# The gates of the experts: scaled one-hot rows made by GpSimd in one step, and the row of numbers read from PSUM by VectorE

## The chip, the cores and the metric

One Trainium2 chip, one core of it. The metric is the device time of one execution in microseconds. The times given are of whole executions; the trace is of one execution more, with its own time beside it.

## What is computed

The program is two blocks of a transformer one after the other, all in float32, for 256 tokens of width 1024. The change lies in the second block, which has two layers. Each ends with a layer of experts: 128 x 128 keys give 16384 experts, and every token picks, for each of 8 heads, 16 of them. From the picks a gate for each token and expert follows.

```python
def peer_ffn(xn, wq, subkeys, u_tab, v_tab):
    ...
    i1 = jnp.take_along_axis(top_i[..., 0, :], ci // PEER_TOPK, axis=-1)
    i2 = jnp.take_along_axis(top_i[..., 1, :], ci % PEER_TOPK, axis=-1)
    idx = i1 * PEER_N_KEYS + i2
    g = jax.nn.softmax(best, axis=-1)
    ...
        act = jax.nn.gelu(jnp.einsum('ckd,cd->ck', u_tab[ic], xc), approximate=False)
        return jnp.einsum('ck,ckd->cd', (gc * act).astype(v_tab.dtype), v_tab[ic])
```

So a token has 8 x 16 = 128 picks, each with a first key, a second key and a weight. The kernel computes every expert's activation and multiplies it by a gate that is the weight where the expert was picked and zero elsewhere.

## The kernel before

Every engine runs its own fixed list of instructions in the order written; semaphores order the engines against each other. A layer of the second block is a `Mixer` and a `Peer`. In `Peer`, these steps follow one another: the norm and the projections of the queries; the scores against the 128 keys of each half; `EarlyScores`, in which TensorE computes the activations of the first 33 of 128 tiles of experts while VectorE runs `Route` (the sixteen best, and the picks); `Gates`; and `Experts`, the long loop over 128 tiles of 128 experts.

`Route` leaves in the tile `slots` three numbers of each pick: with the 128 picks on the partitions and the 256 tokens along a row, `slots[:, 0, n]` is the weight, `slots[:, 1, n]` the first key and `slots[:, 2, n]` the second key of token n.

`Gates` turns them into a matrix of 128 x 128 gates for each token, one matmul per token. For token n it needs two tiles of 128 picks by 128 numbers: `first`, which has a one where the number is the pick's first key, and `second`, which has the weight where the number is the pick's second key. Their product over the picks is the token's gates. Four tokens make a group, whose four products fill one bank of PSUM (banks 0 to 3 in turn); there are 64 groups in a layer, 128 in all. `second` lies in a part of `hT` that is not otherwise in use (the context's half), so that its rows are named hT in the profile. For each group g:

- VectorE, in `make`, compares the row of numbers `iota` (0 to 127, in SBUF) with the second keys of the four tokens (L2441, 128x512) and with the first keys (L2443, 128x512), two instructions.
- ScalarE, in `scale`, multiplies each of the four tokens' rows of `second` by the weight, in place (L2463, four instructions of 128x128).
- TensorE multiplies (L2422; each of the four matmuls in float32 stands as two rows in the trace).
- ScalarE, in `move_late`, moves the gates of 95 of the 128 tiles of experts to `gates` (L2470, 128x380, from PSUM).
- VectorE, in `weigh_early`, multiplies the activations of the first 33 tiles with their gates, read from PSUM (L2449, 128x132).

VectorE's list is make(g), weigh_early(g - 2), and ScalarE's is move_late(g - 2), scale(g). make(g) waits for the products of group g - 4, which used the same one of four buffers; weigh_early(g) waits for move_late(g). GpSimd does nothing in `Peer`; its work is in the attention of the first block (L1239) and in the mixers (L1511, L1602 and others), and its lines for a mixer come before and after it. `Experts` begins on VectorE and ScalarE when the last gates are moved and weighed. Bank 4 was last used for the scores against the keys, and is used next for the sums of `Experts`.

Of the kernel before, what the change touches and what calls it, by code (L numbers as in the profile page):

```python
# [10 lines left out]
ACT = mybir.ActivationFunctionType  # L11
ALU = mybir.AluOpType
AX = mybir.AxisListType

P = 128
# [33 lines left out]
class Span:  # L49


    def __init__(self, sem, first):
        self.sem, self.first = sem, first
# [17 lines left out]
class Use:  # L71
# [3 lines left out]
    def __init__(self, tensor, written, read):  # L75
        self.tensor, self.written, self.read = tensor, written, read
# [11 lines left out]
class Bank:  # L88
    def __init__(self, tensor, written, read):
        self.tensor, self.written, self.read = tensor, written, read  # L90
# [75 lines left out]
def hold(engine, marks):  # L166

    for sem, count in marks:
        engine.wait_ge(sem, count)
# [107 lines left out]
class Fetch:  # L277
# [7 lines left out]
    def scalar(self, after=()):  # L285
        hold(self.nc.scalar, after)
        for dst, src in self.pairs:
            self.nc.scalar.dma_start(dst, src).then_inc(self.landed.sem, 16)
# [7 lines left out]
class Setup:  # L296
# [5 lines left out]
    def vector(self):  # L302
        nc, k = self.k.nc, self.k
        nc.vector.memset(k.ones[:], 1.0).then_inc(self.made.sem, 1)
        nc.vector.memset(k.eps, EPS).then_inc(self.made.sem, 1)
        nc.vector.memset(self.silu[:], 0.0).then_inc(self.made.sem, 1)


class Modulation:
# [35 lines left out]
    def tensor(self, step):  # L345
        k, pe, (g, c) = self.k, self.k.nc.tensor, divmod(step, DC)
        use = self.rows[g]
        if step == 0:
            pe.wait_ge(*self.silu_made.after(1))
        if c == 0:  # L350
            pe.wait_ge(*use.free())
        units = [k.ring.take_whole() for _ in range(2)]
        for b in range(4):
            m = pe.matmul(use.tensor[32 * b:32 * b + 32, :], self.silu[:, c, :],  # L354
                          units[b // 2][:, (b % 2) * 512:(b % 2 + 1) * 512], start=(c == 0), stop=(c == DC - 1))
            if b % 2:
                m.then_inc(k.ring.used, 1)
# [412 lines left out]
class Projection:  # L770


    def __init__(self, k, w, tiles, cuts, x, width, place, arrive=None, b0=0, scale=lambda t: 1.0, between=None):
        self.scale, self.between = scale, between
        self.k, self.w, self.tiles, self.cuts, self.x, self.width = k, w, list(tiles), cuts, x, width
        self.place, self.arrive = place, arrive
        self.first_half = 0
        self.uses = [k.bank[b0 + n % 4].use(written=0) for n in range(len(self.tiles))]
        self.done = [u.emptied() for u in self.uses[-2:]]
# [276 lines left out]
class PairAttention:  # L1056
# [175 lines left out]
    def gpsimd(self):  # L1232
        pool = self.k.nc.gpsimd
        for s in range(len(self.steps)):
            n = self.keys(s)
            pool.wait_ge(*self.den.after(s + 1))
            for u in range(2):
                p = self.prob[:, s % 3, u, 0:n]
                pool.tensor_scalar(p, p, self.rec[:, s % 4, u:u + 1], 1.0, ALU.mult,  # L1239
                                   ALU.mult).then_inc(self.weighed.sem, 1)  # L1240
# [1154 lines left out]
class Gates:  # L2395
# [5 lines left out]
    def __init__(self, k, slots, iota, early, gates, first, second, routed):  # L2401
        self.routed = routed
        self.k, self.slots, self.iota, self.early, self.gates = k, slots, iota, early, gates
        self.first, self.second = first, second
        self.uses = [k.bank[g % 4].use() for g in range(self.GROUPS)]
        self.second_made = k.named("second_key_rows").take(self.GROUPS)
        self.first_made = k.named("first_key_rows").take(self.GROUPS)
        self.scaled = k.named("rows_scaled").take(self.GROUPS)
        self.moved = k.named("gates_moved").take(self.GROUPS)
        self.done = [u.emptied() for u in self.uses[-4:]] + [self.moved.after(self.GROUPS)]  # L2410

# [3 lines left out]
    def tensor(self):  # L2415
        pe = self.k.nc.tensor
        for g, use in enumerate(self.uses):
            pe.wait_ge(*self.first_made.after(g + 1))
            pe.wait_ge(*self.scaled.after(g + 1))
            pe.wait_ge(*use.free())  # L2420
            for t in range(4):
                m = pe.matmul(use.tensor[:, t * P:(t + 1) * P], self.first[:, g % 4, t, :], self.rows(g, t),  # L2422
                              start=True, stop=True)
            m.then_inc(use.written.sem, 1)

    def vector(self):
        hold(self.k.nc.vector, self.routed)
        for g in range(self.GROUPS + 2):
            if g < self.GROUPS:
                self.make(g)  # L2430
            if g >= 2:
                self.weigh_early(g - 2)

    def make(self, g):
        dve = self.k.nc.vector
        row_no = self.iota[:].unsqueeze(1).to_broadcast([P, 4, P])
        tokens = slice(4 * g, 4 * g + 4)
        keys = [self.slots[:, j, tokens].unsqueeze(2).to_broadcast([P, 4, P]) for j in (1, 2)]
        if g >= 4:
            dve.wait_ge(*self.uses[g - 4].full())  # L2440
        dve.tensor_tensor(self.second[g % 4], row_no.rearrange("p (c k) n -> p c k n", c=2),  # L2441
                          keys[1].rearrange("p (c k) n -> p c k n", c=2), ALU.is_equal).then_inc(self.second_made.sem, 1)
        dve.tensor_tensor(self.first[:, g % 4], row_no, keys[0], ALU.is_equal).then_inc(self.first_made.sem, 1)  # L2443

    def weigh_early(self, g):
        dve, use = self.k.nc.vector, self.uses[g]
# [3 lines left out]
                          ALU.mult).then_inc(use.read.sem, 1)  # L2450

    def scalar(self):
        for g in range(self.GROUPS + 2):
            if g >= 2:
                self.move_late(g - 2)
            if g < self.GROUPS:
                self.scale(g)

    def scale(self, g):
        act = self.k.nc.scalar  # L2460
        act.wait_ge(*self.second_made.after(g + 1))
        for t in range(4):
            m = act.activation(self.rows(g, t), self.rows(g, t), ACT.Copy,  # L2463
                               scale=self.slots[:, 0, 4 * g + t:4 * g + t + 1])
        m.then_inc(self.scaled.sem, 1)

    def move_late(self, g):
        act, use = self.k.nc.scalar, self.uses[g]
# [169 lines left out]
class Peer:  # L2638
# [38 lines left out]
    def tensor(self):  # L2677
        pe = self.k.nc.tensor
        self.normed.tensor()
        self.q1.tensor()  # L2680
        self.q2.tensor()
        hold(pe, self.fetch.done + self.q1.done + self.q2.done)
        for tt in range(2):
            for g, use in enumerate(self.key_uses[tt]):
                pe.wait_ge(*use.free())
                for j in range(4):
                    n = 4 * g + j
                    m = pe.matmul(use.tensor[:, j * P:(j + 1) * P], self.qT[:, n, tt * P:(tt + 1) * P],
                                  self.subkeys[:, n, :], start=True, stop=True)
                m.then_inc(use.written.sem, 1)  # L2690
        self.scored.tensor()
        self.route.tensor()
        self.gate.tensor()
        self.experts.tensor()

    def scalar(self):
        act = self.k.nc.scalar
# [23 lines left out]
class Program:  # L2721
# [56 lines left out]
    def gpsimd_program(self):  # L2778
        self.even.gpsimd()
        self.odd.gpsimd()  # L2780
        for layer in self.layers[0::2]:
            layer.gpsimd()


# [153 lines left out]
```

## Time and profile before

| | |
|---|---|
| time, median of 3 executions | 3473.45 us (3460.08 to 3475.53) |
| time of the execution that was profiled | 3467.66 us |
| its span, first to last instruction | 3466.1 us |
| TensorE busy | 3180.4 us, 92% of the span |
| VectorE busy | 2029.0 us, 59% |
| ScalarE busy | 1648.6 us, 48% |
| GpSimd busy | 111.2 us, 3% |
| chain of work that ended last | TensorE 87%, VectorE 6%, issue 4%, ScalarE 3% |

In the rows further on PE is TensorE (PEld its weight loads), DVE is VectorE, ACT is ScalarE and POOL is GpSimd. A row of a group of instructions gives its line in the kernel, the engine, the operation, the names of output and inputs, the shapes, the count, the total busy time in us and the mean duration of one in ns; behind the last bar stands the engine's idle time before them and what ended it. In a timeline the first number is the start from the span's beginning and the second how long the row lasted, both in us.

### The profile page before, as it was taken

What the parts mean: (1) busy time and instruction counts of PE and PEld (TensorE: products, weight loads), DVE (VectorE), ACT (ScalarE), POOL (GpSimd) and SP (SyncE); (2) the same over time, 40 slices, a digit from 0 to 9 for tenths busy, and PEclk for the clock granted to TensorE, in tenths of its full rate; (3) what the DMA queues carried; (4) which work ended last, traced back from release to release, by engine and by line L of the source; (5) the groups of instructions that cost most, each with busy time, mean ns of one, the idle gap of its engine ahead of it and who ended that gap; (6) DMA issues with size and microseconds to landing.
All of it is one profiled execution on the core that took longest, in us unless ns stands there. A gap on an engine that the chain in (4) does not pass through costs nothing.

```text
span 3466.1 us, 50181 instructions
## 1 busy us (share of the span) xinstructions
PE 3180.4 (92%) x18944; PEld 2700.9 (78%) x18944; DVE 2029.0 (59%) x4174; ACT 1648.6 (48%) x3566; POOL 111.2 (3%) x176
## 2 busy tenths in 40 slices
PE   7998999997899878996899999988799679999999
PEld 4745677776799767985789999978698568999998
DVE  2233433335665665689666666657569876666665
ACT  2244322223655335319655555543441875555554
POOL 0022000000200020000000000001100000000000
PEclk9989999998999878999999999989699999999999
DMA  5501444432155313440355655543144025555654
GB/s 212 182 1 68 158 170 169 157 106 80 50 185 178 136 62 95 155 135 1 128 186 187 187 185 188 187 158 111 36 166 152 31 72 185 187 184 188 188 183 152
DMA packets 135055, 479.85 MB, mean 138 GB/s; under 512 B 15520, under 2 KB 17440, under 8 KB 134048
## 3 DMA queue, kind: packets, MB, share of 16 engines
q1 hardware_dynamic: 132944, 471.26, 41.6%
q10 hardware_dynamic: 1872, 5.38, 0.4%
q8 instruction: 153, 2.51, 0.3%
q14 instruction: 86, 0.70, 0.1%
HBM read 475.53 MB, written 1.05 MB: 137 GB/s over the span
## 4 chain that ended last, share of the span: by engine, by line
PE 87%; DVE 6%; issue 4%; ACT 3%; DMA 1%; ACTq 0%; DVEq 0%; SPq 0%
PE psum L763 15%; PE psum L765 14%; PE psum L764 14%; PE psum L2577 7%; PE psum L2579 7%; PE psum L2578 7%; PE psum L2498 7%; PE psum L2422 4%; PE psum L853 2%; PE psum L1112 2%; PE psum L354 1%; PE psum L613 1%; PE psum L1122 1%; PE psum L627 1%; DVE a_scaled L728 1%
## 5 line engine op out<-in xcount | busy, mean ns | idle before, releaser
L248 DVE TENSOR_TENSOR w_lo<-raw,w_hi 128x512 fp32r<-128x512 f32 x1440 | 971.3, 691 | 788.2 <-ACT w_hi L239 760.0
L239 ACT ACTIVATE w_hi<-raw 128x512 fp32r<-128x512 f32 x1440 | 875.1, 625 | 823.2 <-PE psum L765 450.1
L763 PE MATMUL psum<-x_hi,w_hi 128*128 128x256 f32 x2032 | 581.6, 286 | 3.6 <-DVE x_lo L679 3.6
L765 PE MATMUL psum<-x_hi,w_lo 128*128 128x256 f32 x2032 | 580.1, 285 | 0.0
L764 PE MATMUL psum<-x_lo,w_hi 128*128 128x256 f32 x2032 | 576.9, 284 | 0.0
L2577 PE MATMUL psum<-w_hi,wt_hi 128*128 128x512 f32 x1024 | 407.5, 398 | 6.5 <-DVE wt_lo L2635 6.5
L2579 PE MATMUL psum<-w_hi,wt_lo 128*128 128x512 f32 x1024 | 406.0, 396 | 0.0
L2578 PE MATMUL psum<-w_lo,wt_hi 128*128 128x512 f32 x1024 | 405.2, 396 | 0.0
L763 PEld LDWEIGHTS psum<-x_hi,w_hi 128*128 128x128 f32 x2032 | 389.1, 191 | 12.1 <-issue 4.0
L764 PEld LDWEIGHTS psum<-x_lo,w_hi 128*128 128x128 f32 x2032 | 391.9, 193 | 8.0
L765 PEld LDWEIGHTS psum<-x_hi,w_lo 128*128 128x128 f32 x2032 | 387.5, 191 | 0.0
L763 PE MATMUL psum<-a_hi,w_hi 128*128 128x512 f32 (+1 forms) x880 | 310.4, 353 | 17.7 <-DVE a_lo L735 16.3
L765 PE MATMUL psum<-a_hi,w_lo 128*128 128x512 f32 (+1 forms) x880 | 305.5, 347 | 0.0
L764 PE MATMUL psum<-a_lo,w_hi 128*128 128x512 f32 (+1 forms) x880 | 304.2, 346 | 0.0
L2579 PEld LDWEIGHTS psum<-w_hi,wt_lo 128*128 128x128 f32 x1024 | 193.9, 189 | 46.7
L2498 PE MATMUL psum<-xn,u_raw 128*128 128x256 f32 x1056 | 228.2, 379 | 0.0
L2577 PEld LDWEIGHTS psum<-w_hi,wt_hi 128*128 128x128 f32 x1024 | 193.4, 189 | 44.7 <-DVE wt_lo L2635 6.9
L2578 PEld LDWEIGHTS psum<-w_lo,wt_hi 128*128 128x128 f32 x1024 | 194.3, 190 | 38.3
L2422 PE MATMUL psum<-hT,first 128*128 128x128 f32 x1024 | 147.9, 289 | 82.4 <-issue 76.7
L763 PEld LDWEIGHTS psum<-a_hi,w_hi 128*128 128x128 f32 x880 | 168.5, 192 | 70.0 <-issue 37.8
L2498 PEld LDWEIGHTS psum<-xn,u_raw 128*128 128x128 f32 x1056 | 200.5, 190 | 27.2
L2422 PEld LDWEIGHTS psum<-hT,first 128*128 128x128 f32 x1024 | 127.4, 196 | 103.2 <-issue 96.9
(312 smaller groups left out, 4432.3 us busy)
## 6 DMA issues: line engine op xcount, KB each, us to landing
raw<-in_v SPq DMA_DIRECT2D x256, 512.0 KB, 4.4
raw<-in_u SPq DMA_DIRECT2D x190, 512.0 KB, 3.4
raw<-in_mod_w SPq DMA_DIRECT2D x96, 512.0 KB, 4.4
raw<-in_w_gate_up SPq DMA_DIRECT2D x88, 512.0 KB, 4.9
u_raw<-in_u SPq DMA_DIRECT2D x66, 512.0 KB, 3.4
raw<-in_w_in SPq DMA_DIRECT2D x40, 512.0 KB, 3.5
raw<-in_w_down SPq DMA_DIRECT2D x32, 512.0 KB, 3.5
raw<-in_w_peer SPq DMA_DIRECT2D x32, 512.0 KB, 4.2
```

What stands on the lines that cost most here:

```text
L239: self.nc.scalar.activation(self.hi[:, m % 4, :], self.half(m), ACT.Copy).then_inc(self.rounded[m % 4], 1)
L248: self.nc.vector.tensor_tensor(self.lo[:, m % 4, :], self.half(m), self.hi[:, m % 4, :], ALU.subtract).then_inc(self.ready[m % 4], 1)
L763: pe.matmul(out[:, 0:width], hi[:, w], x_hi, start=(c == 0), stop=False)
L764: pe.matmul(out[:, 0:width], hi[:, w], x_lo, start=False, stop=False)
L765: mm = pe.matmul(out[:, 0:width], lo[:, w], x_hi, start=False, stop=(c == total - 1))
L853: m = pe.matmul(use.tensor[:, 0:self.width], w[:, c * P:(c + 1) * P], self.x(c), start=(c == 0), stop=(c == DC - 1))
L1112: m = pe.matmul(use.tensor[:, 0:n], both[u][j][0], both[u][j][1], start=(j == 0), stop=(j == last))
L2422: m = pe.matmul(use.tensor[:, t * P:(t + 1) * P], self.first[:, g % 4, t, :], self.rows(g, t), start=True, stop=True)
L2498: m = pe.matmul(use.tensor[:, 0:LAT], self.raw[:, t % 3, c * P:(c + 1) * P], self.xn[:, c, :], start=(c == 0), stop=(c == DC - 1))
L2577: pe.matmul(out, self.wt_hi[:, s, rows], hi, start=(t == 0), stop=False, skip_group_check=True)
L2578: pe.matmul(out, self.wt_hi[:, s, rows], lo, start=False, stop=False, skip_group_check=True)
L2579: m = pe.matmul(out, self.wt_lo[:, s, rows], hi, start=False, stop=(t == NKEY - 1), skip_group_check=True)
```

## The change

The kernel's three uses of the row of numbers are made in other places. `second` is made and scaled by GpSimd: one `tensor_scalar` for each token, which compares `iota` with the token's second key and multiplies by its weight, both taken as one number per partition. VectorE keeps the comparison for `first`, and reads the row of numbers from bank 4 of PSUM, where TensorE puts it once in a layer, by a matmul with the identity, ahead of the transposes of `Route`. ScalarE's `scale` is gone, so its list in `Gates` is move_late alone. GpSimd's waits are those of `make`: for `slots` at the start, and for the products of group g - 4.

```diff
@@ class Gates
         self.uses = [k.bank[g % 4].use() for g in range(self.GROUPS)]
+
+        self.numbers = k.bank[4].use(read=self.GROUPS)
         self.second_made = k.named("second_key_rows").take(self.GROUPS)
-        self.first_made = k.named("first_key_rows").take(self.GROUPS)
-        self.scaled = k.named("rows_scaled").take(self.GROUPS)
...
         for g, use in enumerate(self.uses):
-            pe.wait_ge(*self.first_made.after(g + 1))
-            pe.wait_ge(*self.scaled.after(g + 1))
+            pe.wait_ge(*self.numbers.emptied(g + 1))
+            pe.wait_ge(*self.second_made.after(g + 1))
             pe.wait_ge(*use.free())
...
+    def tensor_numbers(self):
+        pe = self.k.nc.tensor
+        pe.wait_ge(*self.numbers.free())
+        pe.matmul(self.numbers.tensor[:, 0:P], self.k.ident, self.iota[:], start=True,
+                  stop=True).then_inc(self.numbers.written.sem, 1)
+
+    def gpsimd(self):
+
+        pool = self.k.nc.gpsimd
+        hold(pool, self.routed)
+        for g in range(self.GROUPS):
+            if g >= 4:
+                pool.wait_ge(*self.uses[g - 4].full())
+            for t in range(4):
+                n = 4 * g + t
+                m = pool.tensor_scalar(self.rows(g, t), self.iota[:], self.slots[:, 2, n:n + 1],
+                                       self.slots[:, 0, n:n + 1], ALU.is_equal, ALU.mult)
+            m.then_inc(self.second_made.sem, 1)
+
     def vector(self):
         hold(self.k.nc.vector, self.routed)
+        self.k.nc.vector.wait_ge(*self.numbers.full())
...
     def make(self, g):
-        dve = self.k.nc.vector
-        row_no = self.iota[:].unsqueeze(1).to_broadcast([P, 4, P])
-        tokens = slice(4 * g, 4 * g + 4)
-        keys = [self.slots[:, j, tokens].unsqueeze(2).to_broadcast([P, 4, P]) for j in (1, 2)]
+
+        dve, row = self.k.nc.vector, self.numbers.tensor[:, 0:P]
         if g >= 4:
             dve.wait_ge(*self.uses[g - 4].full())
-        dve.tensor_tensor(self.second[g % 4], row_no.rearrange("p (c k) n -> p c k n", c=2),
-                          keys[1].rearrange("p (c k) n -> p c k n", c=2), ALU.is_equal).then_inc(self.second_made.sem, 1)
-        dve.tensor_tensor(self.first[:, g % 4], row_no, keys[0], ALU.is_equal).then_inc(self.first_made.sem, 1)
+        dve.tensor_tensor(self.first[:, g % 4], row.unsqueeze(1).to_broadcast([P, 4, P]),
+                          self.slots[:, 1, 4 * g:4 * g + 4].unsqueeze(2).to_broadcast([P, 4, P]),
+                          ALU.is_equal).then_inc(self.numbers.read.sem, 1)
...
     def scalar(self):
-        for g in range(self.GROUPS + 2):
-            if g >= 2:
-                self.move_late(g - 2)
-            if g < self.GROUPS:
-                self.scale(g)
-
-    def scale(self, g):
-        act = self.k.nc.scalar
-        act.wait_ge(*self.second_made.after(g + 1))
-        for t in range(4):
-            m = act.activation(self.rows(g, t), self.rows(g, t), ACT.Copy,
-                               scale=self.slots[:, 0, 4 * g + t:4 * g + t + 1])
-        m.then_inc(self.scaled.sem, 1)
+        for g in range(self.GROUPS):
+            self.move_late(g)
...
@@ class Peer
         self.scored.tensor()
+        self.gate.tensor_numbers()
         self.route.tensor()
         self.gate.tensor()
         self.experts.tensor()
+
+    def gpsimd(self):
+        self.gate.gpsimd()
...
@@ class Program
-        for layer in self.layers[0::2]:
+        for layer in self.layers:
             layer.gpsimd()
```

On ScalarE, at the beginning of `Gates` in the first layer, the kernel before has the scales of the first two groups and then moves and scales in turn (the first two rows are the exponential of `Route`).

```order
L2383 ACT_TABLE_LOAD
L2383 ACTIVATE res_162<-res_162 128x2x128
L2463 ACTIVATE hT_49<-hT_49,slots_142 128x128 x8
L2470 ACTIVATE gates_145<-psum 128x4x95
L2463 ACTIVATE hT_49<-hT_49,slots_142 128x128 x4
L2470 ACTIVATE gates_145<-psum 128x4x95
```

At the same place the changed kernel has the 64 moves of the layer and nothing between them, with the first instructions of `Experts` behind.

```order
L2383 ACT_TABLE_LOAD
L2383 ACTIVATE res_162<-res_162 128x2x128
L2477 ACTIVATE gates_145<-psum 128x4x95 x64
L155 ACT_TABLE_LOAD
L155 ACTIVATE gvec_55<-gvec_55 128x1
```

The 256 scales of a layer have left ScalarE's list. On GpSimd, between the last attention step of the first mixer (L1511) and the clearing of the second mixer's padding (L1593), the changed kernel has the 256 instructions of `Gates.gpsimd`; before, the two neighbours followed each other directly.

```order
L1639 TENSOR_TENSOR y_121<-y_121,proj_115 128x512
L1511 TENSOR_SCALAR prob_126<-prob_126,mix_stats_137 128x256 x16
L2441 TENSOR_SCALAR hT_49<-iota_143,slots_142 128x128 x256
L1593 MEMSET pad_179 128x1152
L1618 COPY pad_179<-proj_169 128x2x256
```

So this engine's list has grown by 256 rows in each layer. On VectorE the same place reads before, from the copy of `slots` on:

```order
L2377 COPY slots_142<-psum 128x3x128 x2
L2441 TENSOR_TENSOR hT_49<-iota_143,slots_142 128x2x256
L2443 TENSOR_TENSOR first_146<-iota_143,slots_142 128x512
L2441 TENSOR_TENSOR hT_49<-iota_143,slots_142 128x2x256
L2443 TENSOR_TENSOR first_146<-iota_143,slots_142 128x512
L2441 TENSOR_TENSOR hT_49<-iota_143,slots_142 128x2x256
L2443 TENSOR_TENSOR first_146<-iota_143,slots_142 128x512
L2449 TENSOR_TENSOR early_144<-psum,early_144 128x4x33
```

And in the changed kernel:

```order
L2377 COPY slots_142<-psum 128x3x128 x2
L2459 TENSOR_TENSOR first_146<-psum,slots_142 128x512 x3
L2467 TENSOR_TENSOR early_144<-psum,early_144 128x4x33
L2459 TENSOR_TENSOR first_146<-psum,slots_142 128x512
L2467 TENSOR_TENSOR early_144<-psum,early_144 128x4x33
```

One comparison of each pair has gone from VectorE, and the one that stays has `psum` in place of `iota` as its first input.

## Rows read from the trace of the kernel before

**Rows 1.** The page's first part: busy us, share of the span, instructions.

```profile
PE 3180.4 (92%) x18944; PEld 2700.9 (78%) x18944; DVE 2029.0 (59%) x4174; ACT 1648.6 (48%) x3566; POOL 111.2 (3%) x176
```

**Rows 2.** Busy time of each engine in two stretches of the first layer's gates.

```profile
core 0: us, PE busy (x) PEld busy (x) DVE busy (x) ACT busy (x) POOL busy (x), PEclk, DMA share, GB/s
1552.00:1580.00 28.00, 18.23 (x120) 16.07 (x120) 25.00 (x46) 26.45 (x77) 0.00 (x0) 0.90 0.00 1
1580.00:1640.00 60.00, 38.60 (x274) 32.91 (x272) 55.63 (x104) 60.00 (x174) 0.00 (x0) 1.00 0.00 1
```

**Rows 3.** Timeline of all engines, one group in the middle of the gates.

```profile
1561.90 1.25 ACT L2463 ACTIVATE hT<-hT,slots 128x128 f32<-128x128 f32 x4
1562.15 0.43 DVE L2449 TENSOR_TENSOR early<-psum,early 128x132 f32<-128x132 f32 x1
1562.49 0.68 DVE L2441 TENSOR_TENSOR hT<-iota,slots 128x512 f32<-128x512 f32 x1
1563.04 0.82 ACT L2470 ACTIVATE gates<-psum 128x380 f32<-128x380 f32 x1
1563.10 0.68 DVE L2443 TENSOR_TENSOR first<-iota,slots 128x512 f32<-128x512 f32 x1
...
1563.25 1.13 PE L2422 MATMUL psum<-hT,first 128*128 128x128 f32 x8 [0.63 <-issue]
```

**Rows 4.** Timeline, TensorE's group 56 groups after that of rows 3.

```profile
1661.61 1.13 PE L2422 MATMUL psum<-hT,first 128*128 128x128 f32 x8 [0.62 <-issue]
```

**Rows 5.** Timeline, where the first layer's gates begin.

```profile
1550.13 1.02 PE L2391 MATMUL psum<-cmat,res 128*128 128x128 f32 x6 [3.47 <-DVE res L2371]
1550.71 1.03 DVE L2377 COPY slots<-psum 128x384 f32<-128x384 f32 x2 [0.64 <-PE psum L2391]
1551.84 0.69 DVE L2441 TENSOR_TENSOR hT<-iota,slots 128x512 f32<-128x512 f32 x1
...
1553.95 3.74 PE L2422 MATMUL psum<-hT,first 128*128 128x128 f32 x16 [2.80 <-DVE first L2443]
```

**Rows 6.** Timeline, where they end.

```profile
1665.11 1.13 PE L2422 MATMUL psum<-hT,first 128*128 128x128 f32 x8 [0.62 <-issue]
...
1666.28 0.80 ACT L2470 ACTIVATE gates<-psum 128x380 f32<-128x380 f32 x1 [0.56 <-PE psum L2422]
...
1667.12 0.42 DVE L2449 TENSOR_TENSOR early<-psum,early 128x132 f32<-128x132 f32 x1 [0.93 <-ACT gates L2470]
```

**Rows 7.** Timeline, beginning and end of the second layer's gates.

```profile
2703.19 1.02 DVE L2377 COPY slots<-psum 128x384 f32<-128x384 f32 x2 [0.64 <-PE psum L2391]
...
2819.60 0.42 DVE L2449 TENSOR_TENSOR early<-psum,early 128x132 f32<-128x132 f32 x1 [0.94 <-ACT gates L2470]
```

**Rows 8.** Timeline of GpSimd in the first block's attention.

```profile
203.04 0.93 POOL L1239 TENSOR_SCALAR prob<-prob,stats 128x256 f32<-128x256 f32 x2 [202.60 <-DVE stats L1178]
204.81 1.36 POOL L1239 TENSOR_SCALAR prob<-prob,stats 128x512 f32<-128x512 f32 x2 [0.83 <-DVE stats L1178]
```

**Rows 9.** Groups of GpSimd instructions, each shape apart.

```profile
L1239 POOL TENSOR_SCALAR prob<-prob,stats 128x512 f32<-128x512 f32 x64 | 43.5, 692 | 604.9 <-DVE stats L1178 604.9
...
L1239 POOL TENSOR_SCALAR prob<-prob,stats 128x256 f32<-128x256 f32 x32 | 14.9, 478 | 248.4 <-DVE stats L1178 248.4
L1608 POOL TENSOR_TENSOR y<-y,tap 128x512 f32<-128x512 f32 x4 | 5.1, 1265 | 0.3
...
L1626 POOL COPY pooled<-work 64x256 f32<-64x256 f32 x2 | 0.8, 390 | 0.1
```

**Rows 10.** Timelines: GpSimd beside VectorE, in the mixer and in the attention.

```profile
1288.55 1.40 POOL L1511 TENSOR_SCALAR prob<-prob,mix_stats 128x256 f32<-128x256 f32 x2 [3.46 <-DVE mix_stats L1448]
...
1288.36 0.87 DVE L1458 SCALAR_TENSOR_TENSOR prob<-prob,mix_stats 128x256 f32<-128x256 f32 x2
...
885.85 1.36 POOL L1239 TENSOR_SCALAR prob<-prob,stats 128x512 f32<-128x512 f32 x2 [2.21 <-DVE stats L1178]
...
886.50 0.43 DVE L1290 TENSOR_TENSOR psum<-psum,swa_mask 128x256 f32<-128x256 f32 x1 [0.74 <-PE psum L1112]
```

## Prediction, written before the changed kernel was run

> **What bounds the kernel now.** I first read the page's busy shares [rows 1]: over the whole span TensorE is busy 92% of the time and GpSimd 3%. That average says nothing about the gates, so I next read the busy times of a stretch that holds only gates [rows 2]. There TensorE is busy 38.60 of 60 us, VectorE 55.63, GpSimd nothing, and ScalarE 60.00 of 60. The reader should see that this is a stage with a bound of its own, and that two engines stand close to it.
>
> The timeline says how close [rows 3]. ScalarE's four scales begin at 1561.90 and its move at 1563.04, so the scales take 1.14 us of its time. TensorE's group is at 1563.25, and 56 groups later at 1661.61 [rows 4]: 98.36 / 56 = 1.756 us a group. The move therefore takes the other 0.61 us. VectorE spends 0.61 us from L2441 to L2443 (1562.49 to 1563.10) and 0.34 from L2449 to L2441 (1562.15 to 1562.49). With a second 0.61 for L2443 that is 1.56 us of work in 1.756, and the rest, 0.2, is a wait for the move, whose end frees L2449. TensorE needs 1.13 us a group. So ScalarE bounds the gates, VectorE follows 0.2 us behind, TensorE 0.6 us.
>
> A layer's gates last from the end of the copy of the slots to the end of the last weighing: 1550.71 + 1.03 = 1551.74 [rows 5] to 1667.12 + 0.42 = 1667.54 [rows 6], 115.8 us. In the second layer it is 2704.21 to 2820.02, 115.8 again [rows 7]. That is 231.6 us in all, 6.7% of the span, and the only part of it in which the change does anything.
>
> **What is removed.** ScalarE loses 4 x 64 scales a layer, 1.14 us a group, and keeps 0.61. VectorE loses one comparison of two, 0.61 us a group, and keeps 0.61 + 0.34 = 0.95. Its first input comes from PSUM now. I cost that at nothing, since L2449, with such an input, and the rows of rows 10 with psum as first input last no longer than their sizes ask (0.43 us for 128x256).
>
> **What is added.** On TensorE there is one matmul of 128x128 a layer. It stands behind the early scores and ahead of the transposes, where TensorE sits idle for 3.47 us waiting for VectorE [rows 5]. Six transposes of that size take 1.02 us, so the one is some 0.2 to 0.4 us and hidden. Without that cover it would cost as much, twice. VectorE waits for it once, long after it is done. Bank 4 is free, since the scores that used it were read before `Route` began.
>
> On GpSimd there are 256 instructions of 128x128 a layer. The trace has none of this size, nor one with a comparison or with two numbers per partition. It does have the same operation with two multiplications, one number per partition and one constant. I take not its duration but the distance between two starts, because the instructions overlap: two of 128x256 last 0.93 us together, one of them 0.478, so the second starts 0.452 after the first. For 128x512 it is 1.36 - 0.692 = 0.668 [rows 8, 9]. The slope is 0.216 us per 256 elements, 0.84 ns each. For 128 elements this gives 0.452 - 0.108 = **0.344 us**, the lower bound of the price p of one instruction.
>
> What could be on top of it is the second number per partition. The copy of 256 elements (on 64 partitions), which has none, lasts 0.390 against 0.478 for the operation with one number and two multiplications, so the two together cost 0.088 [rows 9]. A second number costs between nothing and that, which makes the upper bound 0.432. The comparison in place of a multiplication I cannot bound by a close row; the far one is the TENSOR_TENSOR of GpSimd, a different loop, at 1.265 us for 512 elements against 0.692, 1.12 ns more for each element, so 0.143 for 128: p = 0.344 + 0.143 = 0.487. I take **p = 0.37**, nearer the lowest value, because the row for the same operation already carries one number per partition and two arithmetic steps without a slope above 0.84 ns.
>
> **Whether the two engines get in each other's way.** The trace shows both cases [rows 10]. At 1288.55 two GpSimd instructions of 128x256 take 1.40 us together instead of 0.93; beside them runs VectorE's L1458, which has two inputs in SBUF. At 885.85 two of 128x512 take 1.36 us, their usual time, with VectorE's L1290 (psum and SBUF) running beside them. In the changed gates every comparison and weighing of VectorE has psum as one input, so I cost contention at nothing. Had both inputs stayed in SBUF it would be up to 0.47 us for each such meeting.
>
> This is where the Trainium skill is worth a look: "SBUF — State Buffer", section "Who interferes with whom", says that a VectorE instruction with two SBUF inputs contends with a GpSimd instruction that reads SBUF, and one with at most one SBUF input does not. By that rule, the trace agrees with both halves, 1.40 against 0.93 and 1.36 against 1.36.
>
> **The sum.** GpSimd becomes the bound: a group takes 4p = 1.48 us, against 1.13 on TensorE, 0.95 on VectorE and 0.61 on ScalarE. GpSimd may run four groups ahead, so its waits for old products cost nothing while TensorE follows it by one group. One other circle has to be checked. VectorE makes group g + 1 only after it has weighed group g - 2, which needs that group's products and move. From TensorE's start to the move 1.17 (1665.11 to 1666.28), the move 0.84 (to 1667.12), the weighing 0.34, the comparison 0.68 and about 0.06 to TensorE's start, 3.1 us for three groups, 1.03 each [rows 3, 6]. That is under 1.48, so it stays hidden.
>
> A layer's gates are then: 0.10 us until the first instruction (1551.84 after 1551.74), 64 groups of 4p on GpSimd, about 0.1 for the end of the last one and TensorE's start, and a tail from TensorE's last group to the last weighing of 2.43 (1665.11 to 1667.54). So 256p + 2.6 = 94.7 + 2.6 = 97.3 us. Against 115.8 this saves 18.5 a layer and 37.0 in two. The profiled execution took 3467.66 us (its span 3466.1 and 1.6 around it), so the forecast is 3467.7 - 37.0 = **3431 us**, 1.1% less. The median of the three runs is 3473.45, 6 us above the profiled one, and the runs are 15 us apart, so the result may sit some us above the forecast; I leave the sum as it is.
>
> Nothing is given back later, as far as I see. During the gates no transfers run (1 GB/s in rows 2), because the slots for weights are full, and `Experts` starts with the same slots full. TensorE's clock is at 1.00 in the stretch from 1580 to 1640 and 0.90 in the one before [rows 2], a mean of its two levels, 2.4 GHz and 1.2 GHz, in which TensorE was busy 65% of the time; at 1.13 of 1.48 us it will be busy more. I count nothing for this, and a few us in the range.
>
> **The rivals.**
>
> (a) As forecast, GpSimd bounds the gates with p from 0.344 to 0.408: 256p + 2.6 gives 90.7 to 107.0 a layer, so 3417 to 3450 us. Chance 0.73.
>
> (b) GpSimd bounds them, but p is between 0.408 and 0.46, because the second number per partition or the comparison has a full price. With the upper bound 0.432, a layer is 113.2 and the time 3462 us; with 0.46 it is 120.4 and 3477. The break-even is 256p + 2.6 = 115.8, p = 0.442. Chance 0.14. For it speaks that the margin from 0.344 is only 0.098 us an instruction; against it, that the two multiplications together with a number cost 0.088 over a plain copy.
>
> (c) Slower than before: the comparison and two numbers cost as much as a second input, p = 0.487. A layer is 127.3, 11.5 more than before, and the time 3491 us. It decides from p = 0.46 on, since ScalarE, the old bound, no longer helps when GpSimd is the longer one. Chance 0.09. Rows 9 speak for it, in that GpSimd's instructions of two inputs cost nearly double; against it, that these are of one.
>
> The skill has a rule that would also end here: "GPSIMD Engine Reference", sections 3.1 and 4.1, gives about 2.6 cycles per element for an elementwise operation and advises VectorE for them. By its figure, at its clock of 1.2 GHz, an estimate for the 128 elements is 0.28 us over the fixed part, p near 0.52 and a time near 3506 us. The row of TENSOR_SCALAR, at 0.84 ns an element, does not agree, and the same page says that operations of one input run near one element a cycle. So I leave it its share of (c).
>
> (d) GpSimd is faster than its rows say and TensorE or the circle becomes the bound: 1.13 a group, about 1.7 + 63 x 1.13 + 2.4 = 75.3 a layer, 3387 us. This needs p at 0.28, under the intercept of the rows at 128 elements. Chance 0.04.
>
> **Range and chances.** No change within 0.5% (17 us, about what a measurement of this kernel can tell) is a saving under 8.7 a layer, so p above 0.408. Faster by more is (a) and (d), 0.77. Within 0.5% lies between p = 0.408 and 0.476, (b) and a little of (c): 0.15. Slower 0.08. The range goes from 3410, the lower bound of p less a few us between runs, to 3477, the upper end of (b). Outside it lie (c) and (d), 0.13, and some chance in the runs. The likeliest case alone has 3417 to 3450.
>
> **What would show it.** GpSimd busy without idle time in the gates, with starts 0.37 us apart; TensorE's groups 1.48 us apart, waiting for GpSimd's row; ScalarE at about 0.61 to 0.84 of 1.48 and VectorE near 0.95; the gates 97 us long in either layer; and `Experts` as long as before. The forecast is wrong if GpSimd's starts are over 0.41 apart, if the distance varies with VectorE's work (then psum as input does not keep the engines apart), or if the gates get shorter and the rest longer.

## The result, and the profile after

The changed kernel takes 3643.78 us in the median of 4 runs (3637.10 to 3645.67), the kernel before 3472.11 (3460.08 to 3475.53). The ratio is 1.0498, with a 95% interval from 1.0474 to 1.0523. The change makes the kernel 5% slower. The forecast was 3431 us, and the range ended at 3477.

The page's first part, beside [rows 1]: VectorE and ScalarE have lost work as forecast, and GpSimd has gained 396 us.

```profile
PE 3300.6 (91%) x18948; PEld 2806.9 (77%) x18948; DVE 1951.2 (54%) x4046; ACT 1527.3 (42%) x3054; POOL 507.3 (14%) x688
```

The same two stretches of the first layer's gates as in [rows 2]. GpSimd is now the engine without a gap (60.00 of 60 us busy), VectorE fell from 55.63 to 20.16 and ScalarE from 60.00 to 15.31. So the bound moved to where the forecast had it. But TensorE finished fewer instructions in the same time, 158 instead of 274.

```profile
1552.00:1580.00 28.00, 16.38 (x64) 14.29 (x65) 9.11 (x18) 6.45 (x8) 27.97 (x37) 0.50 0.00 0
1580.00:1640.00 60.00, 40.13 (x158) 35.08 (x159) 20.16 (x40) 15.31 (x19) 60.00 (x78) 0.50 0.00 1
```

The groups in order of time, the counterpart of [rows 3, 5]. TensorE's groups begin 3.09 us apart (1558.35, 1561.44), against 1.756 before. GpSimd's row of 30 instructions takes 23.23 us, 0.774 each.

```profile
1551.94 1.89 DVE L2459 TENSOR_TENSOR first<-psum,slots 128x512 f32<-128x512 f32 x3
1552.03 23.23 POOL L2441 TENSOR_SCALAR hT<-iota,slots 128x128 f32<-128x128 f32 x30 [243.40 <-DVE slots L2377]
...
1558.35 2.05 PE L2422 MATMUL psum<-hT,first 128*128 128x128 f32 x8 [1.05 <-issue]
...
1560.43 0.81 ACT L2477 ACTIVATE gates<-psum 128x380 f32<-128x380 f32 x1 [2.29 <-PE psum L2422]
1561.27 0.43 DVE L2467 TENSOR_TENSOR early<-psum,early 128x132 f32<-128x132 f32 x1 [2.08 <-ACT gates L2477]
...
1561.44 2.05 PE L2422 MATMUL psum<-hT,first 128*128 128x128 f32 x8 [1.05 <-issue]
```

All 512 of GpSimd's new instructions, by their line: least, median and greatest duration in ns.

```profile
L2441 POOL TENSOR_SCALAR hT<-iota,slots x512: 784/791/805, 1552.0 to 2991.8; 128x128 f32<-128x128 f32 x171
```

The end of the first layer's gates, which answers to [rows 6], and the copy of `slots` at their beginning.

```profile
1550.83 1.02 DVE L2377 COPY slots<-psum 128x384 f32<-128x384 f32 x2 [0.64 <-PE psum L2391]
...
1750.13 2.05 PE L2422 MATMUL psum<-hT,first 128*128 128x128 f32 x8 [1.05 <-issue]
...
1753.06 0.42 DVE L2467 TENSOR_TENSOR early<-psum,early 128x132 f32<-128x132 f32 x1 [2.67 <-ACT gates L2477]
```

From 1551.85 to 1753.48 is 201.6 us, and the second layer has 201.6 as well. Against 115.8 that is 85.8 more a layer, 171.6 in all. The medians are 171.7 us apart, but the two profiled spans (3643.2 and 3466.1) are 177.1 apart, so 5.5 us of that pair lie outside the gates. Of these, 4.2 are in the stretch between the first layer's gates and the second's: 1036.7 us before, 1040.9 after. The same stretch takes 1037.2 to 1042.7 us in the traces of e2 to e9 below, whatever was done to the gates, so these 4.2 us are a difference between executions and no effect of the change that could be told. The place of the loss is the gates.

The gates can be built from the forecast's own formula with the measured price p = 0.773 us: 256 x 0.773 + 2.6 = 200.5 us. The missing 1.1 us is mostly the tail. It is 3.35 us (1750.13 to 1753.48) in place of 2.43, because TensorE's granted clock is at 0.50 there, the lower of its two levels (1.2 GHz), and its group lasts 2.05 us instead of 1.13.

### The profile page after: what moved, and what is told of

It is laid out like the page before. It is cut to its first block and busy times, and to the rows that moved or that the text cites. A ratio compares the mean times of both kernels' runs of the same rounds, so it can differ in the third digit from the quotient of the medians.

```text
span 3643.2 us, 50063 instructions
## 1 busy us (share of the span) xinstructions
PE 3300.6 (91%) x18948; PEld 2806.9 (77%) x18948; DVE 1951.2 (54%) x4046; ACT 1527.3 (42%) x3054; POOL 507.3 (14%) x688
## 5 line engine op out<-in xcount | busy, mean ns | idle before, releaser
L2441 POOL TENSOR_SCALAR hT<-iota,slots 128x128 f32<-128x128 f32 x512 | 396.0, 791 | 486.7 <-DVE slots L2377 486.7
L2422 PE MATMUL psum<-hT,first 128*128 128x128 f32 x1024 | 262.1, 438 | 140.0 <-issue 140.0
L2422 PEld LDWEIGHTS psum<-hT,first 128*128 128x128 f32 x1024 | 228.1, 328 | 173.9 <-issue 173.9
L2477 ACT ACTIVATE gates<-psum 128x380 f32<-128x380 f32 x128 | 103.1, 806 | 305.1 <-PE psum L2422 305.1
```

The costliest lines, as they stand in the source:

```text
L2441: m = pool.tensor_scalar(self.rows(g, t), self.iota[:], self.slots[:, 2, n:n + 1], self.slots[:, 0, n:n + 1], ALU.is_equal, ALU.mult)
L2477: act.activation(self.gates[:, :, 4 * g:4 * g + 4].rearrange("p k t -> p t k"), use.tensor[:].rearrange("p (t k) -> p t k", t=4)[:, :, EAR ...
```

## Experiments

The question was what makes an instruction cost 0.773 us where 0.344 to 0.487 had been allowed: the comparison (theory C), the second number per partition (theory N), or VectorE running beside it (theory P).

**e1, the instruction by itself.** A small kernel in which GpSimd runs each form eight times, with every other engine at rest, and then the form of the change beside VectorE. It computes nothing of the reference.

```python
pool.tensor_scalar(out(r), src, a, 1.0, ALU.mult, ALU.mult)         # L54
pool.tensor_scalar(out(r), src, a, b, ALU.mult, ALU.mult)           # L57
pool.tensor_scalar(out(r), src, a, 1.0, ALU.is_equal, ALU.mult)     # L60
pool.tensor_scalar(out(r), src, a, b, ALU.is_equal, ALU.mult)       # L63
pool.tensor_scalar(out(r), src, a, None, ALU.is_equal)              # L66
```

> A small kernel of its own, which computes nothing of the reference and returns zeros. GpSimd runs five forms of tensor_scalar, each eight times back to back at 128, 256 and 512 elements, with no other engine at work: multiply by a number per partition and by a constant (the form of L1239), multiply by two numbers, compare with a number and multiply by a constant, compare with one and multiply by another (the form of the change), compare alone. Then the form of the change seven times at 128 elements beside eight comparisons-sized tensor_tensor of VectorE (128x512), once with two SBUF inputs, once with one from PSUM. In the changed kernel the start-to-start distance is 0.774 us at 128 elements, against 0.344 extrapolated from L1239. Theory C (the comparison is the slow part): both forms with two multiplications stay near 0.344, 0.452 and 0.668 us at 128, 256 and 512; every form with a comparison costs about 0.77 at 128. If its price is per element, 0.43 / 128 = 3.4 ns on top of 0.84, so 1.3 us at 256 and 2.4 at 512. Theory N (the second number per partition is the slow part, a fixed price): two numbers cost 0.77, 0.88 and 1.10 us whatever the operation, and the compare with a constant behind it costs 0.344. Theory P (VectorE beside it stretches GpSimd): the form of the change costs under 0.45 alone and 0.77 only beside VectorE.

GpSimd's timeline at 128 and at 512 elements:

```profile
6.87 2.80 POOL L54 TENSOR_SCALAR dst<-src,num 128x128 f32<-128x128 f32 x8 [6.44 <-DVE num L85]
9.77 3.44 POOL L57 TENSOR_SCALAR dst<-src,num 128x128 f32<-128x128 f32 x8
13.30 5.55 POOL L60 TENSOR_SCALAR dst<-src,num 128x128 f32<-128x128 f32 x8
18.96 6.20 POOL L63 TENSOR_SCALAR dst<-src,num 128x128 f32<-128x128 f32 x8
25.26 4.64 POOL L66 TENSOR_SCALAR dst<-src,num 128x128 f32<-128x128 f32 x8
...
64.22 5.36 POOL L54 TENSOR_SCALAR dst<-src,num 128x512 f32<-128x512 f32 x8
69.68 6.00 POOL L57 TENSOR_SCALAR dst<-src,num 128x512 f32<-128x512 f32 x8
75.78 15.80 POOL L60 TENSOR_SCALAR dst<-src,num 128x512 f32<-128x512 f32 x8
91.68 16.44 POOL L63 TENSOR_SCALAR dst<-src,num 128x512 f32<-128x512 f32 x8
```

The start-to-start distance is the row's length less one instruction's duration, divided by 7. At 128 elements the mean durations are 0.371, 0.446, 0.714, 0.789 and 0.600 us, at 512 elements 0.692, 0.766, 1.994, 2.069 and 1.560. It gives:

| form | 128 | 512 | per element |
|---|---|---|---|
| multiply, constant (L54) | 0.347 us | 0.667 us | 0.83 ns |
| multiply by two numbers (L57) | 0.428 | 0.748 | 0.83 |
| compare, times constant (L60) | 0.691 | 1.972 | 3.34 |
| compare, times number (L63) | 0.773 | 2.053 | 3.33 |
| compare alone (L66) | 0.577 | 1.537 | 2.50 |

The 0.773 of the changed kernel is here with all other engines idle, so theory P falls. The second number costs 0.08 us, fixed, at both lengths, so theory N is true only of a fifth of the difference. The comparison costs 0.34 us at 128 elements, and it is a price per element: 2.5 ns more for each. Theory C holds, short of the 3.4 ns it had expected: that slope had been worked out by dividing all of the extra 0.43 us by 128 elements, and 0.08 us of it is the second number's and about 0.02 a fixed part of the comparison (0.344 - 128 x 0.0025).

The last part of e1 has the form of the change seven times beside eight VectorE instructions of 128x512, first with two SBUF inputs, then with one from PSUM.

```profile
120.99 8.73 POOL L72 TENSOR_SCALAR dst<-src,num 128x128 f32<-128x128 f32 x7
...
130.16 5.43 POOL L72 TENSOR_SCALAR dst<-src,num 128x128 f32<-128x128 f32 x7
...
121.04 5.09 DVE L90 TENSOR_TENSOR ddst<-src,other 128x512 f32<-128x512 f32 x8 [114.27 <-POOL dst L69]
130.29 4.88 DVE L90 TENSOR_TENSOR ddst<-ps,other 128x512 f32<-128x512 f32 x8 [4.17 <-POOL dst L69]
```

With the input from PSUM the seven take 5.43 us, 0.773 each, as alone. With both in SBUF they take 8.73, all of the loss in the three that run beside VectorE (1.85, 1.90 and 1.91 us each), while VectorE loses 0.21 us in eight. The Trainium skill ("SBUF — State Buffer", "Who interferes with whom") calls the pair of ports that the two engines share an exclusive lock, and says of VectorE's two-port modes that whoever issues first holds it for the whole instruction. The run agrees that there is exclusion with two SBUF inputs, and shows it one-sided when VectorE's instructions stand back to back.

**e2, the changed kernel without the comparison.** GpSimd multiplies by both numbers; the gates are not the reference's.

```diff
                 m = pool.tensor_scalar(self.rows(g, t), self.iota[:], self.slots[:, 2, n:n + 1],
-                                       self.slots[:, 0, n:n + 1], ALU.is_equal, ALU.mult)
+                                       self.slots[:, 0, n:n + 1], ALU.mult, ALU.mult)
```

> The changed kernel with the comparison on GpSimd replaced by a multiplication (both numbers per partition stay); its gates are not the reference's. Theory C (comparison slow): distance 0.35 to 0.43 us, gates 90 to 113 us a layer, time 3417 to 3462 us. Theory N (second number slow): as the changed kernel, 0.77 us, 3644 us. Theory P (VectorE's work slows GpSimd): 0.77 us too, 3644 us.

Its single execution took 3457.21 us, and the instructions have lost 0.34 us each (the source line, durations in ns):

```profile
L2441 POOL TENSOR_SCALAR hT<-iota,slots x512: 437/447/453, 1546.2 to 2806.9; 128x128 f32<-128x128 f32 x171
```

Their starts are 0.428 us apart, a group takes 4 x 0.428 = 1.71, and the gates last 112.3 us a layer; the formula gives 256 x 0.428 + 2.6 = 112.2. The one changed word is worth 187 us. In the stretch from 1580 to 1630 us GpSimd (the fifth busy time) is without a gap and TensorE's clock is at 1.00:

```profile
1580.00:1630.00 50.00, 32.75 (x232) 28.07 (x232) 30.00 (x59) 24.00 (x30) 50.00 (x118) 1.00 0.00 1
```

This also confirms the rest of the forecast's chain of steps at a p inside its bounds: GpSimd as the bound, the circle through VectorE hidden, nothing given back later.

**e3, the other part of the change alone.** In the kernel before, VectorE reads the row of numbers from bank 4 for both comparisons.

```diff
+        self.k.nc.vector.wait_ge(*self.numbers.full())
...
-        row_no = self.iota[:].unsqueeze(1).to_broadcast([P, 4, P])
+        row_no = self.numbers.tensor[:, 0:P].unsqueeze(1).to_broadcast([P, 4, P])
```

> The kernel before with one part of the change alone: TensorE puts the row of numbers into bank 4, and VectorE reads it from there for both comparisons; ScalarE scales as before and GpSimd does nothing. If a first input from PSUM costs VectorE nothing, as the prediction had it, the comparisons stay at 0.61 us start to start, ScalarE stays the bound at 1.756 us a group and the time is that of before, 3467 to 3475 us. If the input from PSUM cost VectorE more than 0.1 us an instruction it would pass ScalarE, and each 0.1 us beyond that would add 0.2 x 128 = 26 us.

3469.07 us (3464.26 to 3483.27, 10 runs), ratio 1.0002 (0.9988 to 1.0017). The comparison's group of rows and the stretch from 1580 to 1630 us, where ScalarE is still without a gap:

```profile
L2449 DVE TENSOR_TENSOR hT<-psum,slots 128x512 f32<-128x512 f32 x29 | 19.9, 685 | 0.0
```

```profile
1580.00:1630.00 50.00, 32.28 (x230) 27.79 (x231) 46.41 (x86) 50.00 (x144) 0.00 (x0) 1.00 0.00 1
```

685 ns, the duration of the comparison from SBUF. The PSUM row costs nothing, and by itself it brings nothing.

**e4, the changed kernel with the row of numbers in SBUF.**

```diff
-        dve.tensor_tensor(self.first[:, g % 4], row.unsqueeze(1).to_broadcast([P, 4, P]),
+        dve.tensor_tensor(self.first[:, g % 4], self.iota[:].unsqueeze(1).to_broadcast([P, 4, P]),
```

> The changed kernel, with VectorE's comparison reading the row of numbers from SBUF again, so that it has two SBUF inputs beside a GpSimd that reads SBUF. If the two engines exclude each other for the length of an instruction, GpSimd loses up to 0.6 us in each group of 3.09 us, one meeting a group: up to 128 x 0.6 = 77 us more, 3720 us, the extra time seen as one longer instruction in four. If they don't, GpSimd keeps 0.774 us an instruction and the time is 3644 us. Theory C and theory N say nothing else for this run; theory P (that even the PSUM form stretches GpSimd) expects no difference, since it is stretched already.

One execution at 3652.53 us, 8.8 above the changed kernel's median; the gates last 208.3 us a layer instead of 201.6. Neither expectation was right. All of GpSimd's instructions by their line, then two of VectorE's comparisons:

```profile
L2441 POOL TENSOR_SCALAR hT<-iota,slots x512: 779/786/2327, 1550.9 to 3000.3; 128x128 f32<-128x128 f32 x171
```

```profile
1600.09 0.79 DVE L2459 TENSOR_TENSOR first<-iota,slots 128x512 f32<-128x512 f32 x1
...
1603.27 0.79 DVE L2459 TENSOR_TENSOR first<-iota,slots 128x512 f32<-128x512 f32 x1
```

There is exclusion, but for a lone comparison it is short: VectorE's instruction lasts 0.79 us instead of 0.68, and one of GpSimd's in four 0.87 instead of 0.79. Such a meeting costs GpSimd 0.09 us. The greatest duration, 2.33 us, is that of the first instruction of a layer (2.32 in the second), which runs beside three comparisons back to back, as in e1. It accounts for 1.5 of the 6.7 us that a layer's gates gained.

**e5, the same engine and the same count of instructions, without comparing.** VectorE makes both comparisons (row from PSUM) and GpSimd takes ScalarE's scaling, in place.

```diff
-        act.wait_ge(*self.second_made.after(g + 1))
-        for t in range(4):
-            m = act.activation(self.rows(g, t), self.rows(g, t), ACT.Copy,
-                               scale=self.slots[:, 0, 4 * g + t:4 * g + t + 1])
+            pool.wait_ge(*self.second_made.after(g + 1))
+            for t in range(4):
+                m = pool.tensor_scalar(self.rows(g, t), self.rows(g, t), self.slots[:, 0, 4 * g + t:4 * g + t + 1],
+                                       1.0, ALU.mult, ALU.mult)
```

> The kernel before, with GpSimd in place of ScalarE for the scaling and nothing else of it moved: VectorE makes both comparisons (row of numbers from PSUM), and GpSimd multiplies each token's rows of the second tile by one number per partition and a constant, in place. This gives GpSimd the same 512 instructions of 128x128 as the change, without the comparison. Theory that only the comparison (0.34 us an instruction) made the change slow: GpSimd takes 4 x 0.347 = 1.39 us a group, ScalarE 0.61, VectorE 0.61 + 0.61 + 0.34 = 1.56 and bounds; the gates save 0.2 x 64 = 13 us a layer, time 3442 us (3438 to 3450). Rival, that any work of this kind on GpSimd costs more than it seems (the hand-over to TensorE, in place reads): a group stays over 1.7 us and the time is 3465 us or more.

3448.52 us (3439.77 to 3451.93), ratio 0.9944 (0.9927 to 0.9960). VectorE is without a gap, GpSimd at 45.58 of 50:

```profile
1580.00:1630.00 50.00, 36.26 (x257) 31.12 (x258) 50.00 (x97) 26.74 (x33) 45.58 (x129) 1.00 0.00 1
```

The gates last 104.0 us, (104.0 - 2.6) / 64 = 1.58 us a group against the 1.56 expected. Giving GpSimd this work is sound; what makes the change lose is that it got the comparison too.

**e6, e7, e8: GpSimd does as the change has it, for a part of the tokens.** It makes 1, 1.5 and 1.75 tokens of each four on average, each in one step; VectorE compares and ScalarE scales the rest. The tile `second` is laid out anew, so that the first two or three tokens are one regular pattern.

```diff
+    def kept(self, g):
+        return 3                        # e6
+        return 3 - g % 2                # e7
+        return 3 if g % 4 == 0 else 2   # e8
...
+            for t in range(self.kept(g), 4):
+                n = 4 * g + t
+                m = pool.tensor_scalar(self.rows(g, t), self.iota[:], self.slots[:, 2, n:n + 1],
+                                       self.slots[:, 0, n:n + 1], ALU.is_equal, ALU.mult)
+            m.then_inc(self.others.sem, 1)
...
-        for t in range(4):
+        for t in range(self.kept(g)):
             m = act.activation(self.rows(g, t), self.rows(g, t), ACT.Copy,
```

> The change's one-step rows (comparison and scaling on GpSimd) for one token of four; VectorE compares for the other three (128x384) and ScalarE scales three. Row of numbers from PSUM; the second tile is laid out so that three tokens are one regular pattern. By the measured prices: GpSimd 0.773 us a group, ScalarE 3 x 0.286 + 0.61 = 1.47, VectorE 0.48 + 0.61 + 0.34 = 1.43, TensorE 1.13. ScalarE bounds at 1.47, against 1.756: 18 us a layer, 3432 us (3426 to 3440). Rival: VectorE and GpSimd still meet somewhere, or the waits for three producers cost TensorE something, and the group stays above 1.6 us: 3448 us or more.

> As the one-token split, but GpSimd makes one and two tokens in turn, 1.5 of four on average: GpSimd 1.16 us a group, ScalarE 2.5 x 0.286 + 0.61 = 1.33, VectorE 0.41 + 0.61 + 0.34 = 1.36, TensorE 1.13. VectorE bounds at 1.36 if four buffers even out the turns: 25 us a layer, 3417 us (3412 to 3428). If they don't, the group with two tokens on GpSimd (1.55) is waited for, and the mean lies near 1.45: 3430 us.

> GpSimd makes two tokens in three groups of four and one in the fourth, 1.75 on average: GpSimd 1.353 us a group, VectorE 0.375 + 0.61 + 0.34 = 1.33, ScalarE 2.25 x 0.286 + 0.61 = 1.25. GpSimd and VectorE are level at 1.35, so the time is that of the split before within a few us, 3417 us (3410 to 3430); every token more would make GpSimd the bound, and it would rise by 0.19 us a group for each quarter token: the reason why all four tokens lose.

| | time, us | ratio (95%) | gates, us a layer (first / second) | a group, us (first layer) |
|---|---|---|---|---|
| e6 | 3437.45 | 0.9903 (0.9887 to 0.9920) | 97.2 / 97.6 | 1.48 |
| e7 | 3431.38 | 0.9889 (0.9872 to 0.9905) | 94.4 / 94.9 | 1.43 |
| e8 | 3419.29 | 0.9854 (0.9837 to 0.9870) | 90.5 / 90.6 | 1.37 |

The group is the gates' length less 2.6, over 64. The stretch from 1580 to 1630 us in e6, e7 and e8, one fence for each:

```profile
1580.00:1630.00 50.00, 38.74 (x278) 33.26 (x276) 50.00 (x104) 50.00 (x140) 27.03 (x35) 1.00 0.01 1
```

```profile
1580.00:1630.00 50.00, 40.06 (x286) 34.42 (x286) 48.35 (x106) 48.29 (x124) 41.82 (x54) 1.00 0.00 1
```

```profile
1580.00:1630.00 50.00, 41.88 (x300) 35.90 (x298) 49.70 (x113) 48.28 (x123) 50.00 (x65) 1.00 0.00 1
```

e6 came out at the 1.47 that was worked out from prices, with ScalarE without a gap, and VectorE, reckoned at 1.43, without one too. In e7 no engine is full (VectorE 48.35 of 50, GpSimd 41.82), and the mean is 1.43, near the expectation for the case in which four buffers don't even out the groups with one and two tokens. GpSimd waits there 6.8 us in 50 for TensorE's products; which step sets those 1.43 us was not tried. In e8 GpSimd is without a gap (50.00) and the group takes 1.37, close to 7/4 x 0.773 = 1.353. From there, by the price, every quarter of a token more adds 0.19 us; nothing was run between 1.75 tokens and the changed kernel's four, at 4 x 0.773 = 3.09. e5 to e8 are all faster than both kernels, and e8 is the fastest: 1.5% under the kernel before.

**e9, e8 with the row of numbers in SBUF.**

```diff
-        n, row = self.kept(g), self.numbers.tensor[:, 0:P]
+        n, row = self.kept(g), self.iota[:]
```

> The split of e8 (GpSimd makes 1.75 tokens of four), with VectorE reading the row of numbers from SBUF again, in both comparisons. If the change's PSUM row is worth something, it is here, where GpSimd and VectorE are both nearly full. In e1 GpSimd's instruction took 1.85 to 1.91 us in place of 0.79 beside a back-to-back row of VectorE instructions with two SBUF inputs; in e4 a lone one cost GpSimd 0.09 us. Theory that the cost is the lone one's (0.09 a meeting, two meetings a group): GpSimd 1.353 + 0.18 = 1.53 us a group, 3440 us. Theory that each pair of comparisons, which stand back to back, shuts GpSimd out for its whole length (0.98 us): up to 1.353 + 0.98 = 2.33 us a group, 3540 us. Theory that the row's place does not matter: 3419 us as e8.

3490.01 us (3487.84 to 3505.33), ratio 1.0064 (1.0040 to 1.0088), 71 us above e8. The gates last 129.2 and 127.4 us. GpSimd is still without a gap, but in 50 us it finishes 46 instructions where e8 had 65 (the stretch, then its group of rows, in which 1144 is the mean in ns against 787 in e8):

```profile
1580.00:1630.00 50.00, 32.08 (x209) 28.49 (x209) 36.74 (x80) 35.82 (x87) 50.00 (x46) 0.91 0.00 0
```

```profile
L2446 POOL TENSOR_SCALAR hT<-iota,slots 128x128 f32<-128x128 f32 x46 | 52.0, 1144 | 0.0
```

A group takes (129.2 - 2.6) / 64 = 1.98 us, 0.6 more than in e8, between the two expectations (0.18 and 0.98): the two comparisons in a row cost GpSimd about 0.6 us, which is also 1.75 x (1.144 - 0.787). In this split the change's second part, the row in PSUM, is worth 2%.

## Why the prediction was wrong

**The bound and its parts were right.** ScalarE bounded the gates at 1.756 us a group, GpSimd took over, ScalarE and VectorE had the work that was left to them, the matmul into bank 4 was hidden (0.38 us, ahead of a wait of 3.3), and the input from PSUM cost nothing. That last point is shown by e3 (685 ns from either place) and not by the rows given for it, in which 132 elements and 256 both take 0.43 us. The start was right to 0.1 us, and the tail where TensorE kept its clock (2.43 in e2). With the right p the formula gives the gates to 1.1 us.

**The step that failed is the price of one instruction**, in the part on what is added: "The comparison in place of a multiplication I cannot bound by a close row", followed by the choice p = 0.37. The comparison's term had been sized between nothing and 0.143 us; it measured 0.344 (e1: 0.691 - 0.347), and e2 shows that this alone turns the result, 3457 us without it and 3644 with it. The reason given for the low choice was that the row of L1239 "already carries one number per partition and two arithmetic steps without a slope above 0.84 ns". That row could not bear this out: the slope of two multiplications says nothing of the slope of a comparison, and the comparison's is 3.3 ns with the multiplication behind it. The far row, a second input, served as the dearest case, and nothing tied the comparison to it. The forecast's own sign of being wrong came true: starts over 0.41 us apart, at 0.773.

**The second number** was bounded rightly, from nothing to 0.088: it costs 0.081, near the top of the bound, while p = 0.37 had given it and the comparison 0.026 together. With the comparison free, e2 has the time of the forecast's rival (b), not of its likeliest case.

**Contention** was sized rightly at nothing, with the reason that was given: L2459 has psum as an input, and GpSimd's durations lie between 784 and 805 ns over all 512. The 0.47 us set against it, for a meeting with both inputs in SBUF, has no one value: it was 0.09 for a lone comparison (e4), 0.3 each for two in a row (e9), and 0.5 each for three (e4, the first instruction).

**The rivals.** The right one was (c), chance 0.09, in kind: slower, by a comparison dearer than a multiplication, deciding from 0.46 us on. It was priced at 3491 us where 3644 was measured. The estimate that stood beside it, from the Trainium skill ("GPSIMD Engine Reference", sections 3.1 and 4.1), was on the right side of the break-even too, and was set aside by a row of the wrong operation. The runs measure more than its 2.6 cycles: 3.33 ns an element, 4.0 cycles at the clock it states. And its remark that operations of one input run near one element a cycle holds for two multiplications (0.83 ns) and not for a comparison.

**TensorE's clock.** The forecast had TensorE busier in the gates and so no slower. In the changed kernel the granted clock in the gates is 0.50 instead of 1.00 for all of the stretch from 1580 to 1640 us; before it fell, TensorE had been in its early scores until 1547 and then idle for 3.3 us ahead of the transposes of `Route` and 4.1 behind them. Since a group of 2.05 us fits into 3.09, this costs only the tail, 0.9 us a layer. In e2, with a group at 1.71 us, the clock was back at 1.00 in that stretch, as in the kernel before.

## What to carry to other kernels

A price found for an engine's instruction holds for the arithmetic operation that it was found with, and need not hold for another under the same instruction name: here it went from 0.347 to 0.691 us. Before a loop is handed to an engine whose operation no row shows, ask how far the unknown price may go before the result turns: here the margin was 0.10 us on 0.34, and ten lines of a kernel by itself would have settled it (e1). A slower engine can still help if it gets the share that levels it with the others (7 of 16 tokens, 1.5% faster) and not the whole; and the work that GpSimd is good at (multiplying, e5) is not the work it was given.

## What the runs showed of the hardware

- GpSimd's comparison with a number per partition and a multiplication behind it takes 3.33 ns an element between 128 and 512 elements; a comparison alone takes 2.50 and two multiplications 0.83. A second number per partition adds 0.08 us at 128 and at 512 elements alike (e1).
- The exclusion between GpSimd and a VectorE instruction with two SBUF inputs is uneven. A lone VectorE instruction costs GpSimd 0.09 us and itself lasts 0.11 longer (e4), while a back-to-back row of them stretches one GpSimd instruction from 0.79 us to between 1.85 and 1.91 and itself loses 0.21 us in eight (e1). In a full loop it was 0.6 us for two comparisons (e9). With one input from PSUM nothing was lost: GpSimd's instruction took 783 to 807 ns in the changed kernel and in e6 to e8, and 0.79 us alone. Why a lone one costs so little was not tried further.
